# Sixteen key groups of attention's value product in one insertion instead of two

## The reference

```
hn = rmsnorm(h, norm_g[i]); u = hn @ w_in[i]
a_val, a_glu, a_z, q, k, v, b_z = split(u)      # 3 x 1024, 1024, 256, 256, 1024
ya = conformer_conv(a_val, a_glu, ...) * silu(a_z)
yb = window_attention(q, k, v, bias_band, sink[i]) * silu(b_z)
h = h + concat([ya, yb]) @ w_out[i]
e = rmsnorm(p[i] @ w_pe[i], pe_g[i]); h = h + e * sigmoid(h @ w_pg[i])
```

## Time and profile before

| | before |
|---|---|
| median of 3 runs | 2551.93 us (2550.58 to 2551.99) |
| span of the profiled execution | 2549.6 us |
| median of the runs less that span | 2.3 us |
| TensorE busy | 2543.0 us |
| GpSimd busy | 1417.0 us |
| VectorE busy | 1323.9 us |
| ScalarE busy | 981.9 us |

### The profile page before, as it was taken

The page is one execution under the profiler, slowest core; times in us unless marked ns, Lnnn a source line. Parts: engine busy times, 40 slices in busy tenths (PEclk is TensorE's granted clock), DMA queues, the critical chain, the costliest instruction groups (busy, mean ns, idle before and its releaser), DMA issues.

```text
span 2549.6 us, 38612 instructions
## 1 busy us (share of the span) xinstructions
PE 2543.0 (100%) x13968; PEld 2092.2 (82%) x13968; DVE 1323.9 (52%) x2230; ACT 981.9 (39%) x1516; POOL 1417.0 (56%) x1812
## 2 busy tenths in 40 slices
PE   9999999999999999999999999999999999999999
PEld 7888888888888888888888888888888888888887
DVE  7877766530062387777664301634654655522622
ACT  6222365532262341223655312634322666323521
POOL 6555545455565555555444455555666767655554
PEclk9999999999999999999999999999999999999999
DMA  7333243242333333223333432333333323422322
GB/s 259 102 99 97 92 127 113 96 154 94 99 105 127 115 118 98 98 99 99 111 113 103 158 99 91 99 132 114 109 99 125 99 99 99 140 94 96 99 92 106
DMA packets 87617, 284.79 MB, mean 112 GB/s; under 512 B 8592, under 2 KB 24720, under 8 KB 84432
## 3 DMA queue, kind: packets, MB, share of 16 engines
q1 hardware_dynamic: 77856, 277.89, 32.8%
q10 hardware_dynamic: 9648, 5.36, 1.0%
HBM read 269.55 MB, written 16.81 MB: 112 GB/s over the span
## 4 chain that ended last, share of the span: by engine, by line
PE 100%; DVE 0%; issue 0%; ACT 0%; DVEq 0%
PE acc L1577 19%; PE acc L1579 19%; PE acc L1578 19%; PE sc L1579 6%; PE sc L1578 6%; PE sc L1577 6%; PE sc L1601 3%; PE sc L1603 3%; PE acc L1607 3%; PE acc L1603 3%; PE sc L1607 3%; PE acc L1601 3%; PE tr L1577 1%; PE tr L1579 1%; PE tr L1578 1%; PE att L1792 1%
## 5 line engine op out<-in xcount | busy, mean ns | idle before, releaser
L525 POOL TENSOR_TENSOR WL<-raw,WH 128x256 fp32r<-128x256 f32 x1792 | 1402.2, 817 | 1101.8 <-ACT WH L554 1101.5
L554 ACT ACTIVATE WH<-raw 128x1024 fp32r<-128x1024 f32 x450 | 471.9, 1057 | 1172.2 <-PE acc L1579 652.6
L1577 PE MATMUL acc<-XH,WH 128*128 128x512 f32 x2128 | 831.0, 390 | 0.0
L1578 PE MATMUL acc<-XL,WH 128*128 128x512 f32 x2128 | 828.4, 389 | 0.0
L1579 PE MATMUL acc<-XH,WL 128*128 128x512 f32 x2128 | 828.0, 389 | 0.0
L1577 PEld LDWEIGHTS acc<-XH,WH 128*128 128x128 f32 x2128 | 399.4, 188 | 87.2 <-issue 4.5
L1579 PEld LDWEIGHTS acc<-XH,WL 128*128 128x128 f32 x2128 | 399.4, 188 | 83.4
L1578 PEld LDWEIGHTS acc<-XL,WH 128*128 128x128 f32 x2128 | 399.4, 188 | 82.4
L1577 PE MATMUL sc<-XH,WH 128*128 128x512 f32 x640 | 249.0, 389 | 0.0
L1578 PE MATMUL sc<-XL,WH 128*128 128x512 f32 x640 | 249.0, 389 | 0.0
L1579 PE MATMUL sc<-XH,WL 128*128 128x512 f32 x640 | 249.0, 389 | 0.0
(11 more groups left out here) (290 smaller groups left out, 2970.1 us busy)
## 6 DMA issues: line engine op xcount, KB each, us to landing
raw<-in_w SPq DMA_DIRECT2D x450, 512.0 KB, 3.5
h_spill<-H SPq DMA_DIRECT2D x8, 1024.0 KB, 6.4
H<-h_spill SPq DMA_DIRECT2D x8, 1024.0 KB, 7.2
a<-bias_band SPq DMA_DIRECT2D x16, 384.0 KB, 3.9
H<-in_x SPq DMA_DIRECT2D x5, 1024.0 KB, 8.7
Y<-v_spill ACTq DMA_DIRECT2D x16, 256.0 KB, 5.7
bias_band<-bias_line SPq DMA_DIRECT2D x1, 3072.0 KB, 15.4
out<-H SPq DMA_DIRECT2D x3, 1024.0 KB, 8.3
```

Source lines behind the costliest of these rows:

```text
L525: part = pool.tensor_tensor(WL[:, c], raw[:, c], WH[:, c].bitcast(F), ALU.subtract)
L554: act.activation(WH[:, c], raw[:, c], ACT.Copy).then_inc(wh_ready, 1)
L1577: pe.matmul(bank, WH[:, c], xh, start=first, stop=False)
L1578: pe.matmul(bank, WH[:, c], xl, start=False, stop=False)
```

## The change

The value product of a pair is no longer cut in two: `values(pair)` issues all sixteen key groups in steps 6, 12, 18 and 24, directly ahead of the scores of that step. `att_add` falls away, with its 4 adds a pair. `pv_done` now counts 1 a pair, `att_ready` 2. Block 2 of the scores of an even t waits for all four copies; the waits of block 0 and of odd t fall away. The order of the groups is (12, 0 to 11, 13, 14, 15); each group is multiplied as before.

```diff
+VALUE_PAIRS = CT // 2
+VALUES_AT = {6 * (p + 1): p for p in range(VALUE_PAIRS)}
...
-    return [[seen((i + s) % GROUPS_OF) for s in some] for some in ((12, 0, 1, 4, 5, 6), (9, 2, 3, 7, 8, 10, 11, 13, 14, 15))]
+    return [seen((i + s) % GROUPS_OF) for s in (12, 0, *range(1, 12), 13, 14, 15)]
...
-                sp.wait_ge(pv_done, ly * CT + CT)
+                sp.wait_ge(pv_done, ly * VALUE_PAIRS + VALUE_PAIRS)
...
-                    act.wait_ge(pv_done, ly * CT + (2 * pair + 1))
+                    act.wait_ge(pv_done, ly * VALUE_PAIRS + (pair + 1))
                     for i in (1, 3):
                         act.activation(att_part(pair, i), value_bank(i), ACT.Copy).then_inc(att_far, 1)
...
                 def att_out(pair):
-                    dve.wait_ge(pv_done, ly * CT + (2 * pair + 1))
+                    dve.wait_ge(pv_done, ly * VALUE_PAIRS + (pair + 1))
                     for i in (0, 2):
                         dve.tensor_copy(att_part(pair, i), value_bank(i)).then_inc(att_ready, 1)
-
-                def att_add(pair):
-                    dve.wait_ge(pv_done, ly * CT + (2 * pair + 2))
-                    dve.wait_ge(att_ready, 6 * (ly * CT // 2 + pair) + 2)
-                    dve.wait_ge(att_far, 2 * (ly * CT // 2 + pair + 1))
-                    for i in range(4):
-                        dve.tensor_tensor(att_part(pair, i), att_part(pair, i), value_bank(i), ALU.add).then_inc(att_ready, 1)
...
                         elif b == 2 and t >= 2 and t % 2 == 0:
-                            pe.wait_ge(att_ready, 6 * (ly * CT // 2 + t // 2 - 1) + 1)
-                            pe.wait_ge(att_far, 2 * (ly * CT // 2 + t // 2 - 1) + 1)
-                        elif b == 0 and t >= 2 and t % 2 == 0:
-                            pe.wait_ge(att_ready, 6 * (ly * CT // 2 + t // 2 - 1) + 2)
-                            pe.wait_ge(att_far, 2 * (ly * CT // 2 + t // 2))
-                        elif b == 2 and t >= 2:
-                            pe.wait_ge(att_ready, 6 * (ly * CT // 2 + t // 2))
+                            pe.wait_ge(att_ready, 2 * (ly * VALUE_PAIRS + t // 2))
+                            pe.wait_ge(att_far, 2 * (ly * VALUE_PAIRS + t // 2))
...
-                def values(pair, part):
+                def values(pair):
                     t = 2 * pair
-                    if part == 0:
-                        pe.wait_ge(pt_ready, ly * (2 * PAIRS) + 2 * NB * (t + 2))
-                        if t % GQ == 0:
-                            pe.wait_ge(vr_in[t // GQ], 64 * (ly + 1))
-                    else:
-                        pe.wait_ge(scores_taken, ly * (2 * PAIRS) + 2 * NB * min(CT, t + 3))
-                        pe.wait_ge(att_ready, 6 * (ly * CT // 2 + pair) + 2)
-                        pe.wait_ge(att_far, 2 * (ly * CT // 2 + pair + 1))
-                    for n, each in enumerate(zip(*(value_steps(i)[part] for i in range(4)))):
+                    pe.wait_ge(pt_ready, ly * (2 * PAIRS) + 2 * NB * (t + 2))
+                    if t % GQ == 0:
+                        pe.wait_ge(vr_in[t // GQ], 64 * (ly + 1))
+                    pe.wait_ge(scores_taken, ly * (2 * PAIRS) + 2 * NB * (t + 2))
+                    for n, each in enumerate(zip(*(value_steps(i) for i in range(4)))):
...
-                    if n % 6 < 2 and n >= 6:
-                        values(n // 6 - 1, n % 6)
+                    if n in VALUES_AT:
+                        values(VALUES_AT[n])
                     if n % 3 == 0 and n // 3 < CT:
                         scores(n // 3)
```

More of the change, by code:

```diff
@@ L713, in value_copies @@
                     if g:
-                        act.wait_ge(pv_done, ly * CT + CT // 2)
+                        act.wait_ge(pv_done, ly * VALUE_PAIRS + 2)
                     else:
@@ L740, in _ @@
                             act.activation(tl(T, 5), tl(Y, u // 2), ACT.Tanh).then_inc(ln_th, 1)
-                    if n % 6 == 0 and n:
-                        far_out(n // 6 - 1)
+                    if n in VALUES_AT:
+                        far_out(VALUES_AT[n])
                     if n == Z_STEPS - 2:
@@ L1182, in block_turns @@
                     if t >= 2:
-                        dve.wait_ge(pv_done, ly * CT + t // 2 * 2)
+                        dve.wait_ge(pv_done, ly * VALUE_PAIRS + t // 2)
                     for c, b in enumerate(BLOCKS):
@@ L1208, in silu @@
                     if j >= CT:
-                        dve.wait_ge(att_ready, 6 * (ly * CT // 2 + (j - CT) // 2 + 1))
+                        dve.wait_ge(att_ready, 2 * (ly * VALUE_PAIRS + (j - CT) // 2 + 1))
+                        dve.wait_ge(att_far, 2 * (ly * VALUE_PAIRS + (j - CT) // 2 + 1))
                     settle()
@@ L1226, in _ @@
                             stt(tl(T, j % 2), G[j % 2][:, :], 0.5, rs[:, :], ALU.mult, ALU.mult).then_inc(tile_out, 1)
-                    if n % 6 == 0 and n:
-                        att_out(n // 6 - 1)
+                    if n in VALUES_AT:
+                        att_out(VALUES_AT[n])
                     if n == Z_STEPS - 2:
@@ L1231, in _ @@
                             xlow(t, tl(Y, t), x0 + (NT + t + 1))
-                    if n % 6 == 1 and n > 1:
-                        att_add(n // 6 - 1)
                     if n // 3 < CT:
@@ L1792, in values @@
                                 last = pe.matmul(to[:, :, b0 * QB:b1 * QB], Y[rows, c + hh * DH:c + (hh + 1) * DH],
-                                                 turned(hh, k, b0, b1)[rows, :, :], start=n == 0, stop=n == (5, 9)[part])
+                                                 turned(hh, k, b0, b1)[rows, :, :], start=n == 0, stop=n == GROUPS_OF - 1)
                     last.then_inc(pv_done, 1)
```

## The result

The kernel after takes 2569.34 us as the median of 5 runs (2567.79 to 2571.51), the kernel before 2551.19 in the same measurement (5 runs, 2550.58 to 2551.99). The ratio is 1.0070, with an interval of 1.0058 to 1.0081: 18.2 us lost, where 1.9 were to be gained. The profiled execution has a span of 2566.8 us against 2549.6, so 17.2 of them can be looked for in the trace.

A forecast was written before the change was run, and what follows sets the result against it. TensorE, busy 2543.0 of 2549.6 us, was taken to bound the kernel; -3.8 for insertions and +2.0 for the wait gave -1.9 (rounded), so 2550.1 us, range 2547.7 to 2553.0, forecast chance 0.70.

The forecast's parts named there:

- -3.8 for the insertions: TensorE's stream: 8 fewer insertions, none of their matmuls gone, save 2.6 us in pairs 0 to 2 and 1.3 in pair 3.
- pair 3's: Value product of pair 3, where no scores follow: 4.66 us becomes 4.03, 0.63 saved a place, 1.3 in two.
- +2.0 for the wait: Next pair's scores: block 2 waits for all four copies, 0.33 us more in each of six places.
- In one insertion its 20 rounds still run: from first to last start 2.12 us: Part 1's rounds joined to part 0's take 2.18 us against 2.61 before, saving 0.43 us a place in six.
- as though a reserve of queued instructions ran out: Part 1's last rounds slow from 0.06 to 0.11 us; used for an upper end of a further 0.1 us a place.
- Rival B: Long insertion no cheaper: instructions supplied at some 0.11 us a round of 8; only the wait left, +2.0, 2553.9 us; chance 0.13.
- Rival C: Clock falls to 1.2 GHz behind pairs 0 to 2's long small-matmul stretches: 18.6 us in six, 2568.7 us; chance 0.03.
- D: Pair 3's low halves come late for the output projection and TensorE waits; with 3 us, +4.1, 2556.0 us; chance 0.02.
- A: Wait on the copies gained back, or the long insertion keeps its reserve: -3.8, 2548.1 us; chance 0.11.
- E: The change doesn't do what it says, for instance scores no longer following directly; chance next to nothing.
- What costs nothing: VectorE's 32 fewer adds, later copies, ScalarE, GpSimd's subtraction, SP's load and the end-of-stage slack: no gain or loss.

The follow-up runs named there:

- after, 32 later: Kernel after, with long-met waits adding 32 TensorE instructions in layer 0 ahead of the first insertion; 2572.15 us, ratio 1.0082.
- after, loads held: Kernel after, with SP holding back the weight-unit loads that fall into the value products until the product is done; 2561.74 us, ratio 1.0043.
- ten and six: Kernel after, with ten key groups ahead of the step's end and six directly ahead of the scores, no adds, old waits; 2559.55 us, ratio 1.0032.
- eight and eight: Kernel after, with eight key groups four k tiles ahead of the step's end and eight directly ahead of the scores; 2556.2 us, ratio 1.0018.
- after, first copies: Kernel after, with the old waits: block 2 for each engine's first copy, block 0 for the second; 2569.80 us, ratio 1.0065.
- the same, loads held: Kernel after, with both the old waits on the copies and SP holding the weight-unit loads until the product is done; 2560.63 us.
- scores apart: Kernel after, with the next pair's scores issued four k tiles behind the value product instead of directly; 2563.2 us, ratio 1.0044.
- three bursts: Kernel after, with the product in pieces of 5, 5 and 6 key groups, 3 k tiles between, scores 3 behind; 2555.77 us, ratio 1.0018.
- ten and six, loads held: Kernel after, split into ten and six key groups, with SP's unit loads held while a pair's two insertions run; 2553.64 us, ratio 1.0009.
- before, by 42: Kernel before, with long-met waits adding 42 TensorE instructions in layer 0, nothing else changed; 2553.25 us, ratio 1.0007.
- before, by half a block: Kernel before, with long-met waits adding 128 TensorE instructions in layer 0, nothing else changed; 2552.35 us, ratio 1.0003.
- before, by a whole block: Kernel before, with long-met waits adding 256 TensorE instructions in layer 0, nothing else changed; 2551.33 us, ratio 1.0000.

## Why the prediction was wrong

**The account of the whole.** Working from the spans (before 2549.6), with each stall taken from its trace, 1.2 us (rounded from the 1.15 above) for a stretch of half clock inside an insertion and 1.7 in the stream (half of 3.4, an estimate; 1.6 was measured above), the prediction's own terms of -3.8 for the insertions (-1.3 where only pair 3's is saved, +6.0 for 14 more) and +2.0 for the wait (-0.9 where the scores stand apart) where they apply, and -0.5 where the stall that the kernel before itself has is replaced or gone:

```
kernel                    stalls   clock   insertions  wait   old stall   sum    measured
after                      17.3     2.4      -3.8      +2.0     -0.5     +17.4    +17.2
after, 32 later            18.1     4.8      -3.8      +2.0     -0.5     +20.6    +20.4
after, loads held          12.4     0        -3.8      +2.0     -0.5     +10.1    +10.0
ten and six                 5.2     3.4       0         0       -0.5      +8.1     +8.3
eight and eight             2.5     0         0        +2.0     -0.5      +4.0     +3.2
after, first copies        18.0     3.6      -3.8       0       -0.5     +17.3    +19.3
the same, loads held       14.0     0        -3.8       0       -0.5      +9.7     +9.9
scores apart               13.9     3.4      -1.3      -0.9     -0.5     +14.6    +13.6
three bursts                0       0        +6.0      -0.9     -0.5      +4.6     +3.9
ten and six, loads held     2.1     0         0         0       -0.5      +1.6     +2.3
before, by 42               1.8     0         0         0       -0.5      +1.3     +1.1
before, by half a block     1.7     0         0         0       -0.5      +1.2     +1.5
before, by a whole block    0       0         0         0       -0.5      -0.5     -0.6
```

The kernel with the first copies' waits is 2 us off this account (three stretches of half clock, span 2568.9), the others up to 1.0, so the prices aren't good to better than that in every case.

**The step that failed** is "In one insertion its 20 rounds still run: from first to last start 2.12 us". It joined two rows, each measured behind a stretch of large matmuls, and took for granted that the instructions for the sum of both are there as they are for each. The term of the wait for instructions stood at nothing and measured 17.3 us. TensorE runs 256 instructions of small matmuls in 1.8 to 2.1 us; from the end of a block to the moment when the next but one can be used pass 3.0 to 5.1 us (1366.25 to 1369.30; 1263.46 to 1268.55). A burst that crosses one block end may live on what is already there. One of 640 instructions crosses two or three and stalls at the second, the third or both. The row that should have warned stood in the prediction: the last rounds of 64 columns step by 0.11 us and no longer by 0.06, "as though a reserve of queued instructions ran out". I used it to bound a gain, and not to ask what a longer burst would run into. (What slows those last rounds isn't shown; the unstalled product of pair 0 in layer 1 has such rounds too.)

**Rival B** had the right resource and a wrong form. It made the supply a rate, 0.11 us a round, and so found that the long insertion is at worst no cheaper, +2.0. The rounds weren't slower: the product that has no stall takes 3.82 us to the first score, as forecast. What the bursts meet is a block end and, behind it, a round trip. Nothing in the rows of before gave the size except the one stall of 0.5 us, which isn't a bound for 3 us. The bound would have come from the queue "instruction" beside a burst: block size, spacing and delay of the fetches all stand in the trace of before as well.

**Rival C**, the clock, was said to need three stretches after long runs of small matmuls. Two came, but not after those: they stand at the stalls of 2.92 and 3.01 us, and not at the bursts that have none or shorter ones. Over all traces the stalls beside such a stretch have 2.1 us or more, and two of 2.2 and 2.45 us have none. Holding the loads, which shortens the stalls, removes it. It costs some 2.4 us and is a consequence, not the cause. The Trainium skill, TensorE: Matmul & The Clock Gate, Part 1, has the clock fall after an idle spell, as the prediction cited it, and the trace agrees: granted clock 0.54 behind the 2.92 us, and 1.00 up to them.

**The other terms** held, nearly. For pair 0, from 364.94 to 372.82 pass 7.88 us, without the stall 6.46, against 4.00 + 2.61 = 6.61 for the two insertions of before: 0.15 less, where -0.43 + 0.33 = -0.10 was forecast. The entry is 0.31 us, block 2 is at 0.96 instead of 0.97, the weight loads wait up to 0.8 us for the copy (0.75 forecast), and scores to stream is 2.31 (2.3). By the traces with held loads the wait costs 0.28 a place and not 0.33, and in three of the six places a stall takes in part of it, so the +2.0 was somewhat too large. Pair 3 of layer 0 reaches from 522.29 to 527.84. That is 5.55, less 0.227, plus 0.13 for the slow start, less the 1.41 by which its last round starts later than in the product without a stall, 4.04 against the 4.66 of before: 0.62 us saved, where 0.63 were forecast. One reading of the prediction was wrong and went into no sum: the 0.33 us at the end of part 0 is the step to the first score, not to a large matmul. The rows of the timeline for pair 3:

```profile
522.29 0.39 PE L1573 MATMUL acc<-XH,WL 128*128 128x512 f32 x1
...
527.84 0.50 PE L1571 MATMUL acc<-XH,WH 128*128 128x512 f32 x1
```

**D**, the tail, didn't occur: no wait on a low half is listed for the matmuls of the output projection. **A** is refuted by the rows of block 2, **E** by the list of lines: all sixteen key groups stand in 8 insertions. What costs nothing, by the prediction, cost nothing; what it left out was a queue that is in no list of the program's semaphores.

What is not settled: how far the engine's reserve reaches. That a block end in the first few dozen instructions of an insertion does no harm is seen in every run, but the number of instructions that are taken in ahead was not measured by itself. What fills the time between the end of a fetch and the restart isn't known, nor why the same block end stalls in one execution and not in another. Nor was it tried whether another order of the weight loads brings the ten-and-six kernel below the kernel before; the best kernel here is the one before, and the nearest, with 2551.33, is the same with a shift of a whole block.

## What to carry to other kernels

Price a merged burst of small instructions against the instruction queue as well as the semaphores: count its instructions (here 4 for a small fp32 matmul), compare with the block of a fetch (256), and keep a burst at or below one block between stretches of slow instructions; at up to a quarter more, it is a matter of where the block ends fall, and that moves with every instruction added anywhere ahead. When stalls named "issue" appear at odd places of the work, number them by instruction: a common distance of 256 tells more than the lines they stand on. And look at what else uses the DMA engines while a burst runs, since a fetch of 16 KB waits behind a load of 512 KB.

## What the runs showed of the hardware

- A fetch of 16 KB takes 0.9 to 1.4 us at the ten stalls, and TensorE goes on 2.2 to 2.7 us after its start (524.73 to 526.93; 367.40 to 370.12), so there is over a microsecond behind the transfer in which nothing of the fetch is seen to move. I had not expected that part; with the loads held it is up to 2.8 (421.28 to 424.08).
- The fetch starts 0.6 to 1.1 us after a block end with no load in the way (one of ten: 1.7), and up to 2.8 us after it with a weight load under way. This is the difference between a stall of 1 us and one of 3 with half a clock beside it.
- A stretch of 3.4 us at half clock cost 1.15 and 1.4 us where the scores follow (the second from restart to the first large matmul, 3.22 us against 1.80 with the loads held), and 1.6 in large matmuls.
- Two waits on semaphores share one instruction of TensorE's sequencer and a last one stands on the weight load behind them, so that 96 added waits were 32 instructions in the trace; 256 such instructions in the stream left the time as it was (ratio 0.9991 to 1.0009).
